# Delta-rule scan: both units of a head pair turned back to back, the output thread spread over four slots per pair

## The chip, the cores and the metric

One core of one Trainium2 chip runs the whole program. The metric is device time in microseconds of one execution, and the number given is the median over several executions. TensorE (PE in the profile) multiplies matrices into PSUM, and its loads of the stationary operand are listed as PEld. VectorE is DVE, ScalarE is ACT, GpSimd is POOL, SyncE is SP; SyncE issues the transfers of the part changed here. Each engine works through its own list of instructions in order and waits at semaphores that others raise.

## The reference, cut to what matters

The program computes two blocks of a network with some ten stages. The one that changes is the scan of the first block (RWKV branch): six heads of width 64, two directions, 256 context positions and then 2048 positions, each with a 64x64 state per head.

```python
def _rwkv_scan(state, ins, emit):
    r, w, k, v, kk, a = (jnp.moveaxis(z, 1, 0) for z in ins)
    xs = (w, k, v, kk, a, r) if emit else (w, k, v, kk, a)

    def step(S, inp):
        w_t, k_t, v_t, kk_t, a_t = inp[:5]
        sa = jnp.einsum('bhvk,bhk->bhv', S, kk_t)
        S = (S * w_t[:, :, None, :] - sa[..., None] * (kk_t * a_t)[:, :, None, :]
             + v_t[..., None] * k_t[:, :, None, :])
        y = jnp.einsum('bhvk,bhk->bhv', S, inp[5]) if emit else None
        return S, y
```

Context positions only move the state; for the others y is the result.

## The kernel before, in words

`rwkv_scan` (from line 1437) takes 128 positions of all heads and both directions in a pass, as two chunks of 64. There are NS = 18 passes, two for the context and 16 that give outputs. Heads stand in NG = 3 pairs g, and each pair has two units u = 2g and 2g + 1, one per direction (NU = 6). In each pass a small triangular system per head and chunk has to be inverted. This is done in five doubling levels for each of the three pairs, which makes NI = 15 items, and the pass is cut into 15 slots j, one per item. Three threads of work are laid into these slots, and every engine goes through the slots in the same written order, with the loop pass n:

- The **inverse thread** of pass n. In each slot TensorE does `asked` (line 1635, 16 matmuls, 32 at level 1) for item i and then `grown` (line 1661, 16 matmuls) for item i - 1. ScalarE copies what asked made (line 1775), and grown waits for that copy. VectorE takes what grown made with a predicated copy (line 1817), then transposes it for the next level (1823, 1825). An item's asked waits for the transposes of the item three slots before and, since the PSUM tile `inv` has two buffers, for the predicated copy of the item two before (of level 5: its whole result).
- The **output thread** of pass n - 1. For each pair: `solved` (line 1673, 16 matmuls, two ScalarE scalings behind it, lines 1781 and 1784), `moves` (1690, 16 matmuls, then the two VectorE additions into PQ, line 1833), `gains` (1700, 32 matmuls, then ScalarE's GY copy, line 1789). Each waits for what the one before left on the other engine, all through the PSUM tile `db`. After the third pair come two `state` halves (1711, up to 48 matmuls each), each followed by VectorE's additions into S and Y (1841, 1849). Slots 0 to 8 hold these nine groups and slots 9 and 10 the states.
- The **front thread** of pass n + 1. For each of six units: `turned` (line 1606) puts four 128x128 transposes into the PSUM tile `gram`, ScalarE copies them out (lines 1768, 1769), `grams` (1619, 24 matmuls) writes the same tile, and VectorE multiplies it with a mask into TK (line 1810). The next unit's turned waits for that mask. From slot 3 on, turned stands in slots 3, 5, ... 13 and grams in slots 4, 6, ... 14.

GpSimd scales the inputs that turned reads (`scaled`, 1571, tile XE with two buffers, so that it waits for the turned of two units before) and makes the start of the inverse from the masked grams (`start_of`, 1583), one unit at a time. SyncE loads the inputs of pass n + 3 (three buffers X) once VectorE has made PQ of the pair in pass n, and stores Y after both states.

Within a slot TensorE's order is: asked, grown, output group, front group. VectorE's is: predicated copy and transposes, PQ or state, mask. ScalarE's is: copy of asked, solved or gains, copies of turned.

Of the kernel before, what the change touches and what calls it, by code (L numbers as in the profile page):

```python
# [14 lines left out]
P = 128  # L15
# [1421 lines left out]
def rwkv_scan(nc, R, E, masks, levels, eye, ident, YR):  # L1437

    C = HD
    NG = MT_R  # L1440
    NU = 2 * NG
    NCX, NLT = CTX // P, SEQ // P
    NS = NCX + NLT
# [5 lines left out]
    HEADS = [slice(h * HD, (h + 1) * HD) for h in range(2)]  # L1449
    CHUNKS = [slice(c * C, (c + 1) * C) for c in range(2)]  # L1450
    LANES = [(cp, h) for h in range(2) for cp in range(2)]
    FIRST_HALF, SECOND_HALF = 3 * NG, 3 * NG + 1
    FRONTS_AT = 3

    with ExitStack() as ctx:
        s = Scope(nc, ctx, "rsc")
        X = [[s.sb(f"X{b}{u}", [P, 6, P]) for u in range(NU)] for b in range(3)]
# [39 lines left out]
        def front_banks(f):  # L1497

            return (inv[0], inv[1], db, gram, db, gram)[f] if f < NU else gram

        def other(t):

# [21 lines left out]
        with nc.Block() as block:  # L1524
# [44 lines left out]
            @block.gpsimd  # L1569
            def _(pool):  # L1570
                def scaled(n, u):

                    f = n * NU + u
                    x = X[n % 3][u]
                    pool.wait_ge(x_in[n % 3][u], (n // 3 + 1) * (96 if u % 2 == 0 else 64))
                    if f >= 2:
                        pool.wait_ge(tl_full, f - 1)
                    ends = e[:, u, 2 * n:2 * n + 2]
                    nc.gpsimd.tensor_tensor(x[:, X_I, :].rearrange("p (c t) -> p c t", c=2), ey[:].rearrange("p (c t) -> p c t", c=2),
                                            ends.unsqueeze(2).broadcast_to([P, 2, C]), ALU.mult)  # L1580
                    nc.gpsimd.tensor_tensor(XE[u % 2][:], x[:, X_KB:X_KB + 2, :], ends.unsqueeze(2).broadcast_to([P, 2, P]), ALU.mult).then_inc(xe_ready, 1)

                def start_of(n, u):

                    g, d = u // 2, u % 2
                    pool.wait_ge(m4_done, n * NU + u + 1)
                    tk = TK[n % 2][g]
                    nc.gpsimd.tensor_tensor(W[n % 2][g][:, d, :, :], tk[:, K_S0:K_AT - 1:-1, d, :], ey[:].unsqueeze(1).broadcast_to([P, 2, P]),
                                            ALU.add).then_inc(start_ready, 1)

                nc.gpsimd.memset(S[0][:], 0.0).then_inc(zeroed, 1)
                pool.wait_ge(const_in, 16 * 5)
                for n in range(NS):
                    scaled(n, 0)
                    scaled(n, 1)
                    for u in range(NU):
                        start_of(n, u)
                        if u + 2 < NU:
                            scaled(n, u + 2)

            @block.tensor
            def _(pe):
# [3 lines left out]
                def turned(n, u):  # L1606

                    f = n * NU + u
                    x, to = X[n % 3][u], front_banks(f)
                    pe.wait_ge(xe_ready, f + 1)  # L1610
                    if f >= NU:
                        pe.wait_ge(m4_done, f)
                    elif f >= 4:
                        pe.wait_ge(m4_done, f - 1)
                    for j, src in enumerate((x[:, X_AL, :], XE[u % 2][:, 0, :], XE[u % 2][:, 1, :], x[:, X_V, :])):
                        t = nc.tensor.transpose(to[:, 0, j * P:(j + 1) * P], src, idn[:])
                    t.then_inc(tl_full, 1)

                def grams(n, u):

                    f = n * NU + u
                    x, to = X[n % 3][u], front_banks(f)
                    pe.wait_ge(tl_done, f + 1)
                    for cp in range(2):
                        for h in range(2):
                            mm(to[:, h, cp * P:(cp + 1) * P], x[HEADS[h], X_KB + cp, :], alpha_rho(x, h, u, cp))
                    for cp, h in LANES:
                        be = slice(C, P) if cp == 0 else slice(0, C)
                        mm(to[other(CHUNKS[cp]), h, 4 * C:5 * C], x[HEADS[h], X_AL, rows_of(u % 2, CHUNKS[cp])], x[HEADS[h], X_KB + cp, be])
                    for cp, h in LANES:  # L1630
                        be, al = slice(C, P) if cp == 0 else slice(0, C), rows_of(u % 2, CHUNKS[cp])
                        last = mm(to[al, h, 5 * C:6 * C], x[HEADS[h], X_KB + cp, be], x[HEADS[h], X_AL, al])
                    last.then_inc(gram_full, 1)
# [111 lines left out]
                for n in range(NS + 1):  # L1745
                    for j in range(NI):
                        i = n * NI + j
                        if n < NS:
                            asked(i)
                        if 1 <= i <= NS * NI:  # L1750
                            grown(i - 1)
                        if n:
                            g, part = divmod(j, 3)
                            if j < FIRST_HALF:
                                (solved, moves, gains)[part](n - 1, g)
                            elif j <= SECOND_HALF:
                                state(n - 1, j - FIRST_HALF)
                        if j >= FRONTS_AT and n + 1 < NS:
                            u, part = divmod(j - FRONTS_AT, 2)
                            (turned, grams)[part](n + 1, u)  # L1760

            @block.scalar
            def _(act):
                def turned(n, u):
                    f = n * NU + u
                    act.wait_ge(tl_full, f + 1)
                    tk, to = TK[n % 2][u // 2], front_banks(f)[:, 0, :].rearrange("p (a t) -> p a t", a=4)
                    nc.scalar.copy(tk[:, K_AL:K_V + 1, u % 2, :], to)
                    nc.scalar.copy(tk[CHUNKS[1], K_V + 1, u % 2, :], to[CHUNKS[1], 3, :]).then_inc(tl_done, 1)

                def asked(i):
                    n, lev, g = item(i)
                    act.wait_ge(z_full, i + 1)
                    k = 2 if lev == 1 else 1
                    nc.scalar.copy(TK[n % 2][g][:, K_Z:K_Z + k, :, :].rearrange("p a u t -> p u a t"),
                                   inv[i % 2][:, :, 0:k * P].rearrange("p u (a t) -> p u a t", a=k)).then_inc(z_taken, 1)

                def solved(n, g):
                    act.wait_ge(x12_full, n * NG + g + 1)
                    made = db[:, :, 0:2 * P].rearrange("p u (h a k) -> p u h a k", h=2, a=2)  # L1780
                    nc.scalar.mul(XA[g][:], made[:, :, :, 0, :], -1.0)
                    for cp, t in enumerate(CHUNKS):
                        z = other(t)
                        last = nc.scalar.mul(TK[n % 2][g][z, K_V + cp, :, :].rearrange("p u (h k) -> p u h k", h=2), made[z, :, :, 1, :], -1.0)
                    last.then_inc(x12_ready, 1)

                def gains(n, g):
                    act.wait_ge(gy_full, n * NG + g + 1)
                    nc.scalar.copy(GY[:, g, :, :].rearrange("p (c x) k -> p c (x k)", c=2), db[:, :, 0:2 * P]).then_inc(gy_ready, 1)

                act.wait_ge(const_in, 16 * 5)
                for u in range(NU):
                    turned(0, u)
                for n in range(NS + 1):
                    for j in range(NI):
                        if n < NS:
                            asked(n * NI + j)
                        if n and j < FIRST_HALF and j % 3 != 1:
                            (solved, None, gains)[j % 3](n - 1, j // 3)
                        if j >= FRONTS_AT and n + 1 < NS and (j - FRONTS_AT) % 2 == 0:  # L1800
                            turned(n + 1, (j - FRONTS_AT) // 2)

            @block.vector
            def _(dve):
# [49 lines left out]
                for n in range(NS + 1):  # L1854
                    for j in range(NI):
                        i = n * NI + j
                        if 1 <= i <= NS * NI:
                            grown(i - 1)
                        if n and j < FIRST_HALF and j % 3 == 1:
                            moves(n - 1, j // 3)  # L1860
                        elif n and FIRST_HALF <= j <= SECOND_HALF:
                            state(n - 1, j - FIRST_HALF)
                        if j >= FRONTS_AT and n + 1 < NS and (j - FRONTS_AT) % 2:
                            grams(n + 1, (j - FRONTS_AT) // 2)


def hgrn(nc, PT, q0, i0, z0, masks, ident, head_ones, YH):
# [1966 lines left out]
```

## Time and profile before

| | us |
|---|---|
| median of 3 executions | 5530.79 |
| lowest, highest | 5526.96, 5538.92 |
| profiled execution, its own time | 5535.01 |
| span of its profile | 5533.2 |
| TensorE busy | 4917.3 (89%) |
| VectorE busy | 3518.4 (64%) |
| ScalarE busy | 1930.8 (35%) |
| GpSimd busy | 1292.0 (23%) |

The profiled execution lies 4.2 us above the median; its span leaves out 1.8 us around it. The busy shares are means over about ten stages with different limits. The scan lies between about 984 and 1660 us of the span. Busy time of TensorE counts each matmul from its start to its modelled end, so that neighbouring ones overlap. In the timeline, instructions of one line and tile that follow each other closely are one row: its first start, its length until the last end, and the count.

### The profile page before, as it was taken

What the parts mean: (1) busy time and instruction counts of PE and PEld (TensorE: products, weight loads), DVE (VectorE), ACT (ScalarE), POOL (GpSimd) and SP (SyncE); (2) the same over time, 40 slices, a digit from 0 to 9 for tenths busy, and PEclk for the clock granted to TensorE, in tenths of its full rate; (3) what the DMA queues carried; (4) which work ended last, traced back from release to release, by engine and by line L of the source; (5) the groups of instructions that cost most, each with busy time, mean ns of one, the idle gap of its engine ahead of it and who ended that gap; (6) DMA issues with size and microseconds to landing.
All of it is one profiled execution on the core that took longest, in us unless ns stands there. A gap on an engine that the chain in (4) does not pass through costs nothing. (4 is left out here: it accounts for less than half of the span.)

```text
span 5533.2 us, 113254 instructions
## 1 busy us (share of the span) xinstructions
PE 4917.3 (89%) x47505; PEld 3761.5 (68%) x47505; DVE 3518.4 (64%) x5799; ACT 1930.8 (35%) x3321; POOL 1292.0 (23%) x1130
## 2 busy tenths in 40 slices
PE   5999999799987866979998679999897999979989
PEld 2788888677776754858886334444486888766767
DVE  5166566577768874858982678888654000358877
ACT  3244444344435522341112234444304000136642
POOL 4111111222210000350000047677535111000012
PEclk7999999899998988989999779999998999979999
DMA  8244434322211124633324210000364112220145
GB/s 290 82 142 163 142 138 150 107 70 70 71 33 71 57 97 163 196 117 113 109 89 168 96 45 23 19 18 14 113 190 130 69 71 74 95 96 34 41 130 159
DMA packets 506325, 561.09 MB, mean 101 GB/s; under 512 B 114830, under 2 KB 411290, under 8 KB 493802
## 3 DMA queue, kind: packets, MB, share of 16 engines
q1 hardware_dynamic: 435900, 366.30, 21.7%
q10 hardware_dynamic: 54622, 130.36, 6.1%
q0 software_dynamic: 15312, 57.45, 2.6%
q8 instruction: 362, 5.93, 0.4%
q14 instruction: 129, 1.06, 0.1%
HBM read 350.86 MB, written 203.12 MB: 100 GB/s over the span
## 5 line engine op out<-in xcount | busy, mean ns | idle before, releaser
L164 PE MATMUL p_bank<-p_hT_high,p_w_high 128*128 128x512 f32 (+1 forms) x2744 | 1038.8, 379 | 7.8 <-PEq L37 7.8
L165 PE MATMUL p_bank<-p_hT_low,p_w_high 128*128 128x512 f32 (+1 forms) x2744 | 1030.6, 376 | 0.0
L166 PE MATMUL p_bank<-p_hT_high,p_w_low 128*128 128x512 f32 (+1 forms) x2744 | 1030.5, 376 | 0.0
L164 PEld LDWEIGHTS p_bank<-p_hT_high,p_w_high 128*128 128x128 f32 x2744 | 517.8, 189 | 109.6 <-issue 17.5
L166 PEld LDWEIGHTS p_bank<-p_hT_high,p_w_low 128*128 128x128 f32 x2744 | 518.0, 189 | 94.0
L165 PEld LDWEIGHTS p_bank<-p_hT_low,p_w_high 128*128 128x128 f32 x2744 | 518.3, 189 | 92.2
L3076 POOL TENSOR_TENSOR at_acc<-at_acc,at_p 128x512 f32<-128x512 f32 x256 | 414.4, 1619 | 125.0 <-ACT at_p L3012 102.3
L3012 ACT ACTIVATE at_p<-at_sc 128x1024 f32<-128x1024 f32 (+1 forms) x296 | 284.8, 1013 | 379.2 <-PE at_sc L2903 361.4
L3118 DVE TENSOR_REDUCE at_mx<-at_mb 128x2 f32<-128x1024 f32 (+1 forms) x280 | 342.1, 1222 | 51.8 <-PE at_mb L2914 51.5
L164 PE MATMUL o_bank<-o_w_high,o_m_high 128*128 128x512 f32 x800 | 315.3, 394 | 64.1 <-POOL o_m_low L158 64.1
L1050 DVE COPY p_o<-p_bank 128x512 f32<-128x512 f32 (+1 forms) x52 | 33.9, 651 | 466.8 <-PE p_bank L166 466.8
L165 PE MATMUL o_bank<-o_w_low,o_m_high 128*128 128x512 f32 x800 | 314.5, 393 | 0.0
L166 PE MATMUL o_bank<-o_w_high,o_m_low 128*128 128x512 f32 x800 | 314.1, 393 | 0.0
L2935 PE MATMUL at_ob<-at_p,at_V 128*64 128x512 f32 (+1 forms) x1184 | 283.4, 599 | 0.7 <-ACT at_osb L3019 0.7
L1604 PE MATMUL rsc_inv<-rsc_W,rsc_TK 64*64 64x64 f32 x8640 | 253.9, 222 | 8.4 <-DVE rsc_W L1817 6.9
L2902 PE MATMUL at_sc<-at_Q,at_K 128*128 128x512 f32 (+1 forms) x592 | 247.4, 419 | 1.9 <-DMA at_Q<-attention_tops 1.9
L413 ACT COPY p_o<-p_bank 128x512 f32<-128x512 f32 (+1 forms) x147 | 82.2, 560 | 477.8 <-PE p_bank L166 468.4
L1604 PEld LDWEIGHTS rsc_inv<-rsc_W,rsc_TK 64*64 64x64 f32 x8640 | 219.2, 135 | 35.4 <-issue 31.1
L3150 DVE TENSOR_TENSOR at_acc<-at_acc,at_p 128x512 f32<-128x512 f32 x256 | 205.2, 801 | 55.5 <-ACT at_p L3012 49.0
L2903 PE MATMUL at_sc<-at_Q,at_K 128*128 128x512 f32 (+1 forms) x592 | 232.2, 393 | 0.0
L164 PEld LDWEIGHTS o_bank<-o_w_high,o_m_high 128*128 128x128 f32 x800 | 152.2, 190 | 97.0 <-POOL o_m_low L158 65.2
L1134 ACT ACTIVATE p_eo<-p_bank 128x512 f32<-128x512 f32 (+1 forms) x100 | 55.6, 556 | 422.0 <-PE p_bank L166 422.0
(448 smaller groups left out, 9842.3 us busy)
## 6 DMA issues: line engine op xcount, KB each, us to landing
pT<-p_o ACTq DMA_DIRECT2D x128, 256.0 KB, 2.4
rwkv_chunks<-p_arr POOLq DMA_DIRECT2D x54, 512.0 KB, 5.4
o_z<-pT SPq DMA_DIRECT2D x50, 512.0 KB, 5.3
o_y<-y SPq DMA_DIRECT2D x50, 512.0 KB, 6.7
pT<-p_eo ACTq DMA_DIRECT2D x96, 256.0 KB, 2.0
rsc_X<-rwkv_chunks SPq DMA_DIRECT2D x378, 64.0 KB, 2.1
x<-o_o ACTq DMA_DIRECT2D x32, 512.0 KB, 2.7
o_x<-x SPq DMA_DIRECT2D x32, 512.0 KB, 4.6
```

Of the source, the lines that this page charges most:

```text
L164: nc.tensor.matmul(out, lhs[0], rhs[0], start=start, stop=False)
L165: nc.tensor.matmul(out, lhs[0], rhs[1], start=False, stop=False)
L166: return nc.tensor.matmul(out, lhs[1], rhs[0], start=False, stop=stop)
L413: nc.scalar.copy(o[x % NO][:, 0:cnt], ps[c][:, 0:cnt]).then_inc(b_free[c], 1)
L1604: return nc.tensor.matmul(out, l, r, start=start, stop=stop)
L2902: nc.tensor.matmul(sc[t % 2][:, h, 0:n], K1[kv][:, keys], Q1[b % NBUF][:, h, 0:n], start=True, stop=False)
L2903: m = nc.tensor.matmul(sc[t % 2][:, h, 0:n], K2[kv][:, keys], Q2[b % NBUF][:, h, 0:n], start=False, stop=True)
L2935: m = nc.tensor.matmul(ob[h * HD:(h + 1) * HD, 0:n], V[:, tiles[j], kv * HD:(kv + 1) * HD], pr[t % 4][:, h, 0:n], start=(j == 0), stop=(t ...
L3012: nc.scalar.activation(pr[t % 4][:, :, 0:n], sc[t % 2][:, :, 0:n], ACT.Exp, scale=SC).then_inc(exp_done, 1)
L3076: nc.gpsimd.tensor_tensor(acc[b % 2][:, 1, 0:n], acc[b % 2][:, 1, 0:n], pr[t % 4][:, 1, 0:n], ALU.add).then_inc(sum_b, 1)
L3118: r = nc.vector.reduce_max(mx[b % 2][:, :, t:t + nt, c], top_bank(m)[:, :, 0:nt * n].rearrange("p h (j k) -> p h j k", j=nt), AX)
L3150: nc.vector.tensor_tensor(acc[b % 2][:, 0, 0:n], acc[b % 2][:, 0, 0:n], pr[t % 4][:, 0, 0:n], ALU.add).then_inc(sum_a, 1)
```

## The change

The front thread now turns both units of a pair one right after the other, into the two banks of the `gram` tile (`turned_bank`), in slots 2, 6 and 10. Grams follow in slots 3, 4, 7, 8, 11 and 12. The grams of the even unit wait for the copies of both units, and those of the odd unit for the even unit's mask; the next pair's turned waits for the odd unit's mask. The output thread takes four slots per pair: solved, moves, gains in slots 0, 1, 2, then 4, 5, 6, then 8, 9, 10, and the states in slots 11 and 13. Slot 14 has neither. GpSimd scales the two units of the next pair before it makes the starts of this one. The grams' matmuls are as before, the first four of each unit on stationaries of 128 columns.

```diff
--- before.py
+++ after.py
@@ -1449,8 +1449,10 @@
     HEADS = [slice(h * HD, (h + 1) * HD) for h in range(2)]
     CHUNKS = [slice(c * C, (c + 1) * C) for c in range(2)]
     LANES = [(cp, h) for h in range(2) for cp in range(2)]
-    FIRST_HALF, SECOND_HALF = 3 * NG, 3 * NG + 1
-    FRONTS_AT = 3
+    OUTPUTS_AT = [4 * g + part for g in range(NG) for part in range(3)]
+    FIRST_HALF, SECOND_HALF = 4 * NG - 1, 4 * NG + 1
+    TURNED_AT = [4 * g + 2 for g in range(NG)]
+    GRAMS_AT = [4 * g + 3 + u for g in range(NG) for u in range(2)]
 
     with ExitStack() as ctx:
         s = Scope(nc, ctx, "rsc")
@@ -1498,6 +1500,10 @@
 
             return (inv[0], inv[1], db, gram, db, gram)[f] if f < NU else gram
 
+        def turned_bank(f):
+
+            return front_banks(f)[:, 0 if f < NU else f % 2, :]
+
         def other(t):
 
             return slice(C, P) if t.start == 0 else slice(0, C)
@@ -1590,13 +1596,17 @@
 
                 nc.gpsimd.memset(S[0][:], 0.0).then_inc(zeroed, 1)
                 pool.wait_ge(const_in, 16 * 5)
+                scaled(0, 0)
+                scaled(0, 1)
                 for n in range(NS):
-                    scaled(n, 0)
-                    scaled(n, 1)
-                    for u in range(NU):
-                        start_of(n, u)
-                        if u + 2 < NU:
-                            scaled(n, u + 2)
+                    for g in range(NG):
+                        for d in range(2):
+                            if g + 1 < NG:
+                                scaled(n, 2 * g + 2 + d)
+                            elif n + 1 < NS:
+                                scaled(n + 1, d)
+                        for d in range(2):
+                            start_of(n, 2 * g + d)
 
             @block.tensor
             def _(pe):
@@ -1606,21 +1616,27 @@
                 def turned(n, u):
 
                     f = n * NU + u
-                    x, to = X[n % 3][u], front_banks(f)
+                    x, to = X[n % 3][u], turned_bank(f)
                     pe.wait_ge(xe_ready, f + 1)
                     if f >= NU:
-                        pe.wait_ge(m4_done, f)
+                        if u % 2 == 0:
+                            pe.wait_ge(m4_done, f)
                     elif f >= 4:
                         pe.wait_ge(m4_done, f - 1)
                     for j, src in enumerate((x[:, X_AL, :], XE[u % 2][:, 0, :], XE[u % 2][:, 1, :], x[:, X_V, :])):
-                        t = nc.tensor.transpose(to[:, 0, j * P:(j + 1) * P], src, idn[:])
+                        t = nc.tensor.transpose(to[:, j * P:(j + 1) * P], src, idn[:])
                     t.then_inc(tl_full, 1)
 
                 def grams(n, u):
 
                     f = n * NU + u
                     x, to = X[n % 3][u], front_banks(f)
-                    pe.wait_ge(tl_done, f + 1)
+                    if f < NU:
+                        pe.wait_ge(tl_done, f + 1)
+                    elif u % 2 == 0:
+                        pe.wait_ge(tl_done, f + 2)
+                    else:
+                        pe.wait_ge(m4_done, f)
                     for cp in range(2):
                         for h in range(2):
                             mm(to[:, h, cp * P:(cp + 1) * P], x[HEADS[h], X_KB + cp, :], alpha_rho(x, h, u, cp))
@@ -1750,21 +1766,25 @@
                         if 1 <= i <= NS * NI:
                             grown(i - 1)
                         if n:
-                            g, part = divmod(j, 3)
-                            if j < FIRST_HALF:
-                                (solved, moves, gains)[part](n - 1, g)
-                            elif j <= SECOND_HALF:
-                                state(n - 1, j - FIRST_HALF)
-                        if j >= FRONTS_AT and n + 1 < NS:
-                            u, part = divmod(j - FRONTS_AT, 2)
-                            (turned, grams)[part](n + 1, u)
+                            if j in OUTPUTS_AT:
+                                (solved, moves, gains)[j % 4](n - 1, j // 4)
+                            elif j == FIRST_HALF:
+                                state(n - 1, 0)
+                            elif j == SECOND_HALF:
+                                state(n - 1, 1)
+                        if n + 1 < NS:
+                            if j in TURNED_AT:
+                                turned(n + 1, 2 * (j // 4))
+                                turned(n + 1, 2 * (j // 4) + 1)
+                            elif j in GRAMS_AT:
+                                grams(n + 1, GRAMS_AT.index(j))
 
             @block.scalar
             def _(act):
                 def turned(n, u):
                     f = n * NU + u
                     act.wait_ge(tl_full, f + 1)
-                    tk, to = TK[n % 2][u // 2], front_banks(f)[:, 0, :].rearrange("p (a t) -> p a t", a=4)
+                    tk, to = TK[n % 2][u // 2], turned_bank(f).rearrange("p (a t) -> p a t", a=4)
                     nc.scalar.copy(tk[:, K_AL:K_V + 1, u % 2, :], to)
                     nc.scalar.copy(tk[CHUNKS[1], K_V + 1, u % 2, :], to[CHUNKS[1], 3, :]).then_inc(tl_done, 1)
 
@@ -1795,10 +1815,11 @@
                     for j in range(NI):
                         if n < NS:
                             asked(n * NI + j)
-                        if n and j < FIRST_HALF and j % 3 != 1:
-                            (solved, None, gains)[j % 3](n - 1, j // 3)
-                        if j >= FRONTS_AT and n + 1 < NS and (j - FRONTS_AT) % 2 == 0:
-                            turned(n + 1, (j - FRONTS_AT) // 2)
+                        if n and j in OUTPUTS_AT and j % 4 != 1:
+                            (solved, None, gains)[j % 4](n - 1, j // 4)
+                        if j in TURNED_AT and n + 1 < NS:
+                            turned(n + 1, 2 * (j // 4))
+                            turned(n + 1, 2 * (j // 4) + 1)
 
             @block.vector
             def _(dve):
@@ -1856,12 +1877,14 @@
                         i = n * NI + j
                         if 1 <= i <= NS * NI:
                             grown(i - 1)
-                        if n and j < FIRST_HALF and j % 3 == 1:
-                            moves(n - 1, j // 3)
-                        elif n and FIRST_HALF <= j <= SECOND_HALF:
-                            state(n - 1, j - FIRST_HALF)
-                        if j >= FRONTS_AT and n + 1 < NS and (j - FRONTS_AT) % 2:
-                            grams(n + 1, (j - FRONTS_AT) // 2)
+                        if n and j in OUTPUTS_AT and j % 4 == 1:
+                            moves(n - 1, j // 4)
+                        elif n and j == FIRST_HALF:
+                            state(n - 1, 0)
+                        elif n and j == SECOND_HALF:
+                            state(n - 1, 1)
+                        if j in GRAMS_AT and n + 1 < NS:
+                            grams(n + 1, GRAMS_AT.index(j))
 
 
 def hgrn(nc, PT, q0, i0, z0, masks, ident, head_ones, YH):
```

## Rows read from the trace of the kernel before

**Rows 1.** Windows: us, busy us (instructions) of PE, PEld, DVE, ACT, POOL, clock, DMA.

```profile
984.00:1020.00 36.00, 16.08 (x176) 12.21 (x180) 4.79 (x5) 5.09 (x12) 9.50 (x18) 0.55 0.62 177
...
1055.00:1600.00 545.00, 500.40 (x15308) 433.78 (x15306) 421.97 (x1048) 253.17 (x612) 154.92 (x281) 1.00 0.26 68
```

**Rows 2.** Waits of TensorE in the steady scan, 1060 to 1600: total, times, longest.

```profile
PE rsc_gram L1616 <- DVE rsc_TK L1810: 18.5, 31, 0.7
```

**Rows 3.** Timeline of TensorE, one pass: start us, us, line, count, idle before.

```profile
1326.05 0.41 PE L1604 MATMUL rsc_inv<-rsc_W,rsc_TK 64*64 64x64 f32 x16
...
1326.94 0.23 PE L1604 MATMUL rsc_inv<-rsc_W,rsc_TK 64*64 64x64 f32 x2
...
1327.80 0.46 PE L1604 MATMUL rsc_inv<-rsc_W,rsc_TK 64*64 64x64 f32 x16 [0.20 <-DVE rsc_W L1817]
...
1331.36 1.20 PE L1604 MATMUL rsc_db<-rsc_TK 128*64 128x64 f32 x32 [0.53 <-DVE rsc_PQ L1833]
1332.49 0.91 PE L1604 MATMUL rsc_inv<-rsc_W,rsc_TK 64*64 64x64 f32 x32
...
1338.88 0.33 PE L1616 MATMUL rsc_gram<-rsc_idn,rsc_X 128*128 128x128 f32 x1
...
1339.27 0.27 PE L1616 MATMUL rsc_gram<-rsc_idn,rsc_X 128*128 128x128 f32 x1
1339.47 0.86 PE L1604 MATMUL rsc_inv<-rsc_W,rsc_TK 64*64 64x64 f32 x30
...
1340.75 1.11 PE L1604 MATMUL rsc_gram<-rsc_X 64*128 64x128 f32 x24
1341.68 0.70 PE L1604 MATMUL rsc_inv<-rsc_W,rsc_TK 64*64 64x64 f32 x26
...
1345.07 1.20 PE L1604 MATMUL rsc_db<-rsc_TK 128*64 128x64 f32 x32 [0.56 <-DVE rsc_PQ L1833]
...
1347.13 0.87 PE L1604 MATMUL rsc_inv<-rsc_W,rsc_TK 64*64 64x64 f32 x32
1347.84 0.87 PE L1604 MATMUL rsc_db<-rsc_S,rsc_PQ 64*64 64x64 f32 x24
...
1349.33 0.33 PE L1616 MATMUL rsc_gram<-rsc_idn,rsc_X 128*128 128x128 f32 x1
...
1352.17 1.11 PE L1604 MATMUL rsc_gram<-rsc_X 64*128 64x128 f32 x24
1353.09 0.87 PE L1604 MATMUL rsc_inv<-rsc_W,rsc_TK 64*64 64x64 f32 x32
1354.45 0.30 PE L1616 MATMUL rsc_gram<-rsc_idn,rsc_X 128*128 128x128 f32 x1 [0.49 <-DVE rsc_TK L1810]
...
1355.01 0.92 PE L1604 MATMUL rsc_inv<-rsc_W,rsc_TK 64*64 64x64 f32 x32
1356.03 1.11 PE L1604 MATMUL rsc_gram<-rsc_X 64*128 64x128 f32 x24
1356.95 0.87 PE L1604 MATMUL rsc_inv<-rsc_W,rsc_TK 64*64 64x64 f32 x32
1358.55 0.30 PE L1616 MATMUL rsc_gram<-rsc_idn,rsc_X 128*128 128x128 f32 x1 [0.72 <-DVE rsc_TK L1810]
...
1361.05 0.41 PE L1604 MATMUL rsc_inv<-rsc_W,rsc_TK 64*64 64x64 f32 x16
```

**Rows 4.** Timeline of ScalarE, same pass: behind the gains of slot 5.

```profile
1338.99 0.59 ACT L1789 COPY rsc_GY<-rsc_db 128x512 f32<-128x512 f32 x1 [1.19 <-PE rsc_db L1604]
1339.58 0.59 ACT L1768 COPY rsc_TK<-rsc_gram 128x512 f32<-128x512 f32 x1
1340.17 0.26 ACT L1769 COPY rsc_TK<-rsc_gram 64x128 f32<-64x128 f32 x1
```

**Rows 5.** Timeline of VectorE, same pass: mask of slot 6, PQ of slot 7.

```profile
1341.93 0.96 DVE L1810 TENSOR_TENSOR rsc_TK<-rsc_gram,rsc_mk 128x768 f32<-128x768 f32 x1
...
1344.26 0.76 DVE L1833 TENSOR_TENSOR rsc_PQ<-rsc_db,rsc_X 128x256 f32<-128x256 f32 x2
```

## The prediction, made before the changed kernel was run

> **What bounds the kernel now.** Only the delta-rule scan changes, so I first asked for busy time by stretch [rows 1]. In the 545 us of steady scan TensorE is busy 500 us at a granted clock of 1.00, VectorE 422, ScalarE 253, GpSimd 155. "Busy 500" isn't work, since the records of pipelined matmuls overlap; the question is how often TensorE's next group starts late. The waits [rows 2] show one such place by name, the turned tiles behind VectorE's mask: 31 times, 0.6 us each. The timeline of one pass then gives the rest [rows 3]. Passes repeat: 1326.05 to 1361.05 is 35.00 us, 15 slots. I took from it what each group costs when it doesn't wait, from its start to the start of the next:
> - asked + grown (in every slot): 0.70 (1347.13 to 1347.84, rounded down)
> - with the solved group behind them 1.28 (1339.47 to 1340.75)
> - gains 1.13 (1331.36 to 1332.49)
> - one half of the state 1.49 (1347.84 to 1349.33)
> - turned 0.59 (1338.88 to 1339.47)
> - grams 0.93 (1340.75 to 1341.68, and 1352.17 to 1353.09).
>
> Then the late starts. Slot 11: ready at 1353.09 + 0.70 = 1353.79, turned at 1354.45: 0.66 late. Slot 13: 1356.95 + 0.70 = 1357.65, turned at 1358.55: 0.90 late. Slot 12: 1355.01 + 0.70 = 1355.71, grams at 1356.03: 0.32 late, behind ScalarE's copy, and slot 14 is built like it. Together 2.2 us in a pass: the front thread (turned, copy, grams, mask, next turned) has no output group beside it there. The change removes these. The gains of slots 2 and 8 also start late, for PQ (the bracketed 0.53 and 0.56 are only the visible part).
>
> **The change part by part**, walked through a new pass from 0.
>
> *Slots 0 to 2.* Same groups in the same order up to the end of the first gains: 1326.05 to 1332.49, 6.44 us [rows 3]. The change takes nothing out here.
>
> *Turned, twice, behind the gains (slots 2, 6, 10).* Per pass it is six groups as before. TensorE then needs asked and grown, and wants grams of the even unit, which now wait for BOTH copies, and ScalarE has the gains' GY copy before them in its queue. The existing chain is [rows 4]: gains end on TensorE 1338.88, GY from 1338.99, turned's copies from 1339.58 to 1340.17 + 0.26 = 1340.43, 1.55 after the gains' end. A second pair of copies repeats 1340.43 - 1339.58 = 0.85 plus some 0.03 between, and a copy is seen by TensorE 0.06 after it ends: 1.55 + 0.88 + 0.06 = 2.50 us from the gains' end to grams. TensorE's own work in that time is two turned (1.03, below), asked and grown 0.70: 1.73. A new wait of 0.77, in slots 3 and 7; behind it asked and grown of the next slot stand as well. In slot 11 the half state (1.49) covers it.
> The two turned without anything between: from first to last transpose 1338.88 to 1339.27, 0.39, spaced 0.11 after the first, and 0.20 from the last to the next group. So 0.39 + 0.11 + 0.33 + 0.20 = 1.03 where two single ones take 1.18. In slots 2 and 6 ScalarE decides the end, so this counts once in a pass.
> That saving has a rule behind it: the Trainium skill's "TensorEngine Tiling (Array Packing)", Key Properties, says that changing the tiling mode drains TensorE, and a turned is a 128x128 group between 64-row groups. Counted by the rule alone the change would save 0.15 three times instead of once, and the end would be some 5 us earlier; the copies' rows speak against that.
>
> *Grams to grams.* The odd unit's grams wait for the even unit's mask. That chain exists now as grams to the next turned: 1352.17 to 1354.45, 2.28 us [rows 3]. Cover in slots 3 to 4 is 0.93 + 1.28 (asked, grown, solved) = 2.21, so 0.07 is left. In slots 11 to 12 it is 0.93 + 0.70, so 0.65.
>
> *Odd grams to gains.* The new order puts moves in slot 5 and gains in slot 6 behind grams of slot 4. VectorE takes them in order: mask, copy and transposes of a level, PQ. The same order exists in slots 6 to 8 now: grams 1340.75, mask at 1341.93 [rows 5], PQ 1344.26 + 0.76 = 1345.02, gains at 1345.07: 4.32 us. Nothing in it was waiting for TensorE longer than for VectorE (the mask starts right after the grams), so I take 4.32 again, though TensorE has one turned (0.59) less to do in it and so waits longer. It happens twice now (gains of pairs 1 and 2) instead of once. In the old pass the gains of pair 1 hardly waited, since their mask came behind PQ.
>
> *Slots 13 and 14.* Slot 14 holds asked and grown only. The next asked needs the predicated copy of what that grown made. The price is in slot 0 to 1: last grown matmul 1326.94, asked 1327.80, 0.86 with the solved group in between, so solved hid 0.4 of it. Now nothing hides it.
>
> *Sum of a pass.* Slots 0 to 2: 6.44. Then twice (2.50 + 2.28 + 4.32 + 1.13 = 10.23): 20.46. Then turned twice 1.03, asked and grown 0.70, state 1.49, grams to grams 2.28, grams 0.93, asked and grown 0.70, state 1.45, asked and grown 0.70, wait 0.85: 10.13. In all 37.03 against 35.00: **2.0 us longer**. There are 16 passes with outputs and fronts: 32.5 us. The pass without outputs gains nothing and loses about 0.4 (bare slots in the middle), the two context passes have shorter states and lose about 0.1 more each, the last loop pass without fronts gives back 0.2. The tail has the same chain in both. **+33 us.**
>
> *Costed at nothing.* GpSimd: the same two kinds of instructions in another order; it is busy 155 of 545 us [rows 1], and the start tiles of the last pair are ready two slots earlier than now. SyncE: loads for the pass after next but one are released by PQ of pairs 1 and 2, one and two slots later, and the output store behind the second half state three slots later; all are needed a whole pass (35 us) on. If that cover were gone, each late load would hold up turned. The grams' matmuls (24 per unit) don't change at all, and the prologue only swaps a GpSimd order.
>
> *Bounds of the unseen.* The new neighbours moves-asked and state-asked were in no row; they lie beside waits, so between 0 and -0.15 each. The second pair of copies: between 0.85 (back to back) and 1.3, if the level's copy slipped ahead, which the program's order excludes; I take 0.88. The slot 14 wait: between 0.4 (part hidden) and 0.9. Per pass that is -0.7 to +0.5, in all -11 to +8.
>
> **The rivals.**
> 1. *Faster.* The front thread is the only thing that matters: 2.2 us of late starts leave each pass and the new waits don't come, because the four slots per pair give VectorE time. 16 x 2.2 = 35 us less, 5496. For it: these waits are the ones the profile names [rows 2]. Its point of decision is slot 6: PQ would have to be done 3.0 us after the odd grams' start; rows 3 and 5 show 4.32. Chance 5 in 100.
> 2. *No change.* The gains' waits fall to today's size in one of the two pairs and slot 14's is hidden by the asked group's first half: 2.2 gone, about as much new. 5531 +- 11. For it: VectorE has 123 us of slack in 545. Against: this slack lies in other slots. Chance 7.
> 3. *More waits than I see, the same kind:* the slots' asked groups too wait for VectorE's backlog, another 1 us per pass: 5580. Chance 12.
> 4. *The clock.* The granted clock is 1.00 with 4 transposes at a time and gaps under 1 us [rows 1]; before the scan, from 984 to 1020, with little matmul work, it is 0.55. If eight transposes and a 0.8 us wait let it drop to the lower level (1.2 GHz) around each pair, turned twice, asked, grown and grams (1.03 + 0.70 + 0.93 = 2.66) would take double, 8 us per pass, 128 us more: about 5690. The Trainium skill's "TensorE: Matmul & The Clock Gate", Part 4, says that transposes don't count as activity for the clock. Six turned per pass at 1.00 now speak against its mattering. Chance 2.
>
> That the change doesn't do what it says is no rival: the order of the groups is written out, and the wait conditions follow it. Only "128-column stationaries" changes no instruction.
>
> **How the numbers follow.** The forecast (74 in 100): the profiled execution took 5535.0 us, 4.2 above the median of the runs shown, so 5535.0 + 33 = 5568 for it and 5530.8 + 33 = **5564** for the median. Its own range is -11 to +8 from the unseen costs and some 6 of scatter between runs: 5550 to 5577. With the third rival the range is 5547 to 5582; it leaves out the first two and the clock. A measurement of this kernel can tell 0.2%, 11 us, from no change. Slower by more than that: forecast, rivals 3 and 4: 0.88. Within: 0.07. Faster: 0.05.
>
> **What would show it.** Right: a pass of 37.0 us; no wait of turned for the mask; in slots 3 and 7 grams 2.5 us after the gains' end, released by the copy L1769; gains of pairs 1 and 2 at 4.3 us after the odd grams' start, released by PQ; asked of slot 0 with 0.85 us before it. Wrong: a pass at or under 35.2; PQ less than 3.5 us behind the grams; a granted clock under 0.95 in the steady stretch; turned waiting for GpSimd.

## The result and the profile after

The changed kernel takes 5564.84 us in the median of 6 runs (5556.26 to 5570.34), the kernel before beside it 5533.68 (5523.72 to 5544.09, 6 runs). The ratio is 1.0055 with a 95% interval of 1.0039 to 1.0071: slower by 0.55%, clear of the 0.2% that can be told from nothing. The forecast was 5564 in 5547 to 5582. So the total is right, but it holds two items that nearly cancel and that the forecast had put at nothing or had no term for; they come below.

The steady scan, by windows (us, busy us of PE, PEld, DVE, ACT, POOL, granted clock, DMA share, GB/s), answers to [rows 1]:

```profile
1055.00:1600.00 545.00, 460.61 (x14238) 404.65 (x14233) 392.45 (x977) 239.14 (x571) 147.35 (x264) 0.99 0.25 65
```

In the same 545 us TensorE got through 14238 matmuls where it was 15308 before, 7% fewer, at nearly the same clock. Each pass with outputs has the same matmuls, so a pass takes longer. All waits of TensorE in the steady scan (total us, times, longest) answer to [rows 2]:

```profile
PE rsc_inv L1614 <- DVE rsc_W L1838: 28.4, 63, 0.6
PE rsc_db L1614 <- DVE rsc_PQ L1854: 27.2, 41, 0.8
PE rsc_gram L1614 <- ACT rsc_TK L1789: 15.9, 29, 0.5
PE rsc_gram L1614 <- DVE rsc_TK L1831: 5.8, 14, 0.6
PE rsc_inv L1614 <- issue: 5.6, 5, 1.5
```

Of two of these waits the kernel before had smaller ones, beside the row in [rows 2]:

```profile
PE rsc_db L1604 <- DVE rsc_PQ L1833: 16.8, 31, 0.6
PE rsc_inv L1604 <- DVE rsc_W L1817: 3.0, 15, 0.2
```

The old wait, turned (L1616 before, L1627 now) for the mask, is gone as the change meant it to be. Four new or grown ones stand in its place: asked for VectorE's predicated copy (3.0 before, 28.4 now), gains for PQ (16.8 before, 27.2 now), grams for ScalarE's copies, and the odd grams for the even unit's mask. The fifth, "issue", names no releaser.

One pass on TensorE (start us, length, line, count, idle before and its releaser), which answers to [rows 3]:

```profile
1382.24 0.46 PE L1614 MATMUL rsc_inv<-rsc_W,rsc_TK 64*64 64x64 f32 x16 [0.63 <-DVE rsc_W L1838]
...
1388.63 0.33 PE L1627 MATMUL rsc_gram<-rsc_idn,rsc_X 128*128 128x128 f32 x1
...
1389.66 0.92 PE L1614 MATMUL rsc_inv<-rsc_W,rsc_TK 64*64 64x64 f32 x32
1391.12 1.11 PE L1614 MATMUL rsc_gram<-rsc_X 64*128 64x128 f32 x24 [0.55 <-ACT rsc_TK L1789]
...
1393.31 1.11 PE L1614 MATMUL rsc_gram<-rsc_X 64*128 64x128 f32 x24
...
1396.07 0.92 PE L1614 MATMUL rsc_inv<-rsc_W,rsc_TK 64*64 64x64 f32 x32 [0.53 <-DVE rsc_W L1838]
1397.75 1.20 PE L1614 MATMUL rsc_db<-rsc_TK 128*64 128x64 f32 x32 [0.77 <-DVE rsc_PQ L1854]
1398.88 0.33 PE L1627 MATMUL rsc_gram<-rsc_idn,rsc_X 128*128 128x128 f32 x1
...
1409.13 0.33 PE L1627 MATMUL rsc_gram<-rsc_idn,rsc_X 128*128 128x128 f32 x1
...
1412.40 1.11 PE L1614 MATMUL rsc_gram<-rsc_X 64*128 64x128 f32 x24
...
1414.59 1.11 PE L1614 MATMUL rsc_gram<-rsc_X 64*128 64x128 f32 x24 [0.39 <-DVE rsc_TK L1831]
1415.52 0.87 PE L1614 MATMUL rsc_inv<-rsc_W,rsc_TK 64*64 64x64 f32 x32
...
1419.13 0.46 PE L1614 MATMUL rsc_inv<-rsc_W,rsc_TK 64*64 64x64 f32 x16 [0.64 <-DVE rsc_W L1838]
```

The pass is 1419.13 - 1382.24 = 36.89 us. It reads as the walk had it, section by section (predicted in brackets): slots 0 to 2 up to the end of the gains 6.39 (6.44); gains' end to grams 1391.12 - 1388.63 = 2.49 (2.50); grams to grams 2.19 (2.28); odd grams to gains 1397.75 - 1393.31 = 4.44 (4.32); gains 1.13 (1.13); the next pair the same, 1398.88 to 1409.13 = 10.25 (10.23); the rest of the pass 10.00 (10.13). The two turned in a row take 1389.66 - 1388.63 = 1.03, as predicted.

ScalarE and VectorE in that pass show why. ScalarE (same columns), behind the gains, answers to [rows 4]:

```profile
1388.74 0.58 ACT L1809 COPY rsc_GY<-rsc_db 128x512 f32<-128x512 f32 x1 [1.29 <-PE rsc_db L1614]
1389.33 0.58 ACT L1788 COPY rsc_TK<-rsc_gram 128x512 f32<-128x512 f32 x1
1389.93 0.26 ACT L1789 COPY rsc_TK<-rsc_gram 64x128 f32<-64x128 f32 x1
1390.21 0.58 ACT L1788 COPY rsc_TK<-rsc_gram 128x512 f32<-128x512 f32 x1
1390.81 0.26 ACT L1789 COPY rsc_TK<-rsc_gram 64x128 f32<-64x128 f32 x1
```

The five run with hardly a gap (0.03 us at most) from 1388.74 to 1391.07, and grams start 0.05 later, at 1391.12. VectorE answers to [rows 5]:

```profile
1394.62 0.96 DVE L1831 TENSOR_TENSOR rsc_TK<-rsc_gram,rsc_mk 128x768 f32<-128x768 f32 x1
1395.50 0.43 DVE L1838 COPY_PREDICATED rsc_W<-rsc_lv,rsc_inv 128x256 f32<-128x256 uint32 x1
...
1396.94 0.76 DVE L1854 TENSOR_TENSOR rsc_PQ<-rsc_db,rsc_X 128x256 f32<-128x256 f32 x2
```

Mask, the level's copy and transposes, PQ: 3.08 us in one line from 1394.62, and the gains start 0.05 after its end. TensorE has nothing else that its order allows.

### The profile page after: what moved, and what is told of

Same layout as the page of the kernel before. It is cut to its first block and busy times, and to the rows that moved or that the text cites. A ratio compares the mean times of both kernels' runs of the same rounds, so it can differ in the third digit from the quotient of the medians.

```text
span 5561.0 us, 113203 instructions
## 1 busy us (share of the span) xinstructions
PE 4907.5 (88%) x47505; PEld 3757.5 (68%) x47505; DVE 3514.4 (63%) x5799; ACT 1932.5 (35%) x3321; POOL 1294.9 (23%) x1130
## 3 DMA queue, kind: packets, MB, share of 16 engines
q14 instruction: 130, 1.06, 0.1%
## 5 line engine op out<-in xcount | busy, mean ns | idle before, releaser
L1614 PE MATMUL rsc_inv<-rsc_W,rsc_TK 64*64 64x64 f32 x8640 | 257.9, 222 | 43.8 <-DVE rsc_W L1838 38.6
L1838 DVE COPY_PREDICATED rsc_W<-rsc_lv,rsc_inv 128x256 f32<-128x256 uint32 x270 | 118.6, 439 | 153.1 <-PE rsc_inv L1614 150.0
```

The source lines that it names most:

```text
L1614: return nc.tensor.matmul(out, l, r, start=start, stop=stop)
L1838: made = nc.vector.copy_predicated(wt[:, :, 0, :], lv[:, lev, :, 0, :].bitcast(mybir.dt.uint32), new)
```

## The experiments

Passes are given from the second half of a pass's first asked (its matmuls `rsc_inv<-rsc_TK`) to that of the next. In each profile I take the commonest value among the passes that give outputs.

**e1, the pair without the slots.** The changed kernel, GpSimd's new order included, with the output thread where it was (ScalarE's and VectorE's loops change alike; TensorE's is shown):

```diff
-    OUTPUTS_AT = [4 * g + part for g in range(NG) for part in range(3)]
-    FIRST_HALF, SECOND_HALF = 4 * NG - 1, 4 * NG + 1
+    FIRST_HALF, SECOND_HALF = 3 * NG, 3 * NG + 1
...
-                            if j in OUTPUTS_AT:
-                                (solved, moves, gains)[j % 4](n - 1, j // 4)
+                            if j < FIRST_HALF:
+                                (solved, moves, gains)[j % 3](n - 1, j // 3)
```

> The changed kernel with the output thread back in slots 0 to 10 (solved, moves, gains in nine slots running, states in 9 and 10). Walk theory: turning both units together is the costly half. Walked with the same durations a pass takes 36.3 us, between before (35.0) and the changed kernel (36.9), and the kernel is about 21 us slower than before less what the start gains (6 us). Rival (four slots per pair are the costly half, since they leave slot 14 bare and put gains behind the mask): a pass of about 35, and no difference from before.

Measured: 5551.06 us against 5534.79, ratio 1.0030 (1.0017 to 1.0042), passes of 36.3. Both are what the walk gave (36.3 and 15 us net). Turning both units together, alone, adds 1.4 us to a pass, where the whole change adds 2.0.

**e2, the slots without the pair.** The kernel before with the output thread on the new slots on all engines, GpSimd and fronts as they were (the engines' loops, which follow these lists, are left out, in e4 too):

```diff
-    FIRST_HALF, SECOND_HALF = 3 * NG, 3 * NG + 1
+    OUTPUTS_AT = [0, 1, 2, 4, 5, 6, 8, 9, 10]
+    FIRST_HALF, SECOND_HALF = 11, 13
```

> The kernel before with only the output thread on four slots per pair (states in 11 and 13); fronts one unit at a time in slots 3 to 14, GpSimd's order as before. Walk theory: this half alone helps a little, since slots 11 and 13 get the states as cover for the mask: a pass of 34.7 us, the kernel 5 us faster, which the clock can't tell from no change. Rival (the output slots are the costly half): a pass of 36 or more, 15 us or more slower.

Measured: 5529.13 against 5534.79, ratio 0.9986 (0.9976 to 0.9996), passes of 34.6. A pass is 0.3 shorter than before. So the slots alone help a little, and it is only with the pair that they hurt: 36.9 with both, 36.3 with the pair alone. The two halves don't add up. It isn't the mask in front of PQ that the pair adds: e2 has that too, in both pairs, from the grams of slot 4 to the gains of slot 6 and from slot 8 to 10 (in the first 1296.37 to 1300.68, 4.31 us), and its gains wait 24.1 us for PQ in all, where the changed kernel's wait 27.2. What e2 hasn't got is any wait of the grams for ScalarE's copies (15.9 in the changed kernel), and its asked waits 3.0 us for the predicated copy and not 28.4. In e2 a turned stands between those grams and gains, under VectorE's chain; with the pair none does, and the asked and the gains wait instead.

**e3, grams one slot later.** The changed kernel with

```diff
-    GRAMS_AT = [4 * g + 3 + u for g in range(NG) for u in range(2)]
+    GRAMS_AT = [4 * g + 4 + u for g in range(NG) for u in range(2)]
```

> The changed kernel with both grams of a pair one slot later (slots 4, 5, 8, 9, 12, 13). Walk theory: the copies have ended when grams come, and the odd mask no longer stands before PQ on VectorE: a pass of 34.9 us against 36.9, 2.0 less, so about as fast as before. Rival (only the wait for the two copies costs): 1.5 less, 35.4. Rival (the pair's eight transposes and ScalarE's load cost whatever follows): 36.5 or more.

Measured: 5530.83 against 5534.79, ratio 0.9996 (0.9986 to 1.0005), passes of 35.0: 1.9 shorter than the changed kernel, from one line. It is the length that the theory gave (34.9) and not that of the copies' wait alone (35.4), and the transposes or ScalarE's load, both unchanged, can't hold 1.9 us. TensorE, from the first gains to the next:

```profile
1291.50 0.33 PE L1627 MATMUL rsc_gram<-rsc_idn,rsc_X 128*128 128x128 f32 x1
...
1294.08 0.93 PE L1614 MATMUL rsc_inv<-rsc_W,rsc_TK 64*64 64x64 f32 x30 [0.64 <-DVE rsc_W L1838]
...
1295.44 1.11 PE L1614 MATMUL rsc_gram<-rsc_X 64*128 64x128 f32 x24
...
1297.62 1.11 PE L1614 MATMUL rsc_gram<-rsc_X 64*128 64x128 f32 x24
1298.55 0.87 PE L1614 MATMUL rsc_inv<-rsc_W,rsc_TK 64*64 64x64 f32 x32
1299.75 0.46 PE L1614 MATMUL rsc_db<-rsc_TK 128*64 128x64 f32 x8 [0.33 <-DVE rsc_PQ L1854]
```

These gains end at 1300.88, so from the end of one pair's gains to that of the next it is 9.38 us where the changed kernel has 10.25. This comes twice in a pass; the rest of the pass gives 0.15. The grams' wait for the copies (0.55 visible) is gone, but the asked ahead of them now waits 0.64 for the predicated copy, so nothing is won there. What is won lies behind the grams: the wait of slot 6's asked (0.53) is gone, and the gains wait 0.33 for PQ and not 0.77. Between a pair's even grams and its PQ VectorE now has one mask to do and not two; the odd unit's mask comes behind PQ. Two rows of TensorE's waits:

```profile
PE rsc_inv L1614 <- DVE rsc_W L1838: 35.2, 62, 0.8
PE rsc_db L1614 <- DVE rsc_PQ L1854: 15.9, 42, 0.5
```

The gains' wait for PQ fell from 27.2 to 15.9 us, and the wait of grams for ScalarE (15.9) isn't among the rows any more. The wait of asked for VectorE has grown in its place (28.4 to 35.2), in the slot between turned and grams that is now bare.

**e4, other slots.** The same walk, used to look for a better order. The kernel before with

```diff
-    FIRST_HALF, SECOND_HALF = 3 * NG, 3 * NG + 1
-    FRONTS_AT = 3
+    OUTPUTS_AT = [0, 1, 2, 3, 4, 6, 7, 8, 10]
+    FIRST_HALF, SECOND_HALF = 12, 13
+    TURNED_AT, GRAMS_AT = [2, 4, 6, 8, 10, 12], [3, 5, 7, 9, 11, 14]
```

> The kernel before with other slots: outputs in 0, 1, 2, 3, 4, 6, 7, 8, 10, states in 12 and 13, turned one unit at a time in 2, 4, 6, 8, 10, 12, grams in 3, 5, 7, 9, 11, 14. Walk theory: nearly every mask and copy has another group beside it, a pass takes 32.7 us against 35.0, 16 times 2.3 is 37 us less: 5495. Rival (TensorE's own issue is the bound at about 35 once waits are moved, or late instruction fetches grow as it issues faster): a pass of 34 or more, less than 16 us gained.

Measured: 5505.35 against 5534.79, ratio 0.9939 (0.9922 to 0.9955), 29 us less. The steady scan by windows, and TensorE's waits there:

```profile
1055.00:1600.00 545.00, 520.47 (x16106) 453.03 (x16103) 445.39 (x1109) 268.94 (x643) 157.14 (x284) 1.00 0.26 68
```

```profile
PE rsc_inv L1605 <- DVE rsc_W L1821: 6.4, 21, 1.1
PE rsc_db L1605 <- DVE rsc_PQ L1837: 5.3, 11, 0.5
PE rsc_inv L1605 <- issue: 2.5, 6, 1.1
PE rsc_db L1605 <- issue: 1.9, 4, 0.7
```

16106 matmuls in the window, 5% more than before. One pass goes from 1244.54 to 1277.30, 32.76 us; the walk had 32.7. But other passes of it take up to 34.3, and the mean of fourteen is 33.1. The 37 us expected came out as 29 mostly for that reason. The rows hold 4.4 us of "issue", waits with no releaser; that late instruction fetches are behind them is not shown. The rival as it stood, a pass of 34 or more and less than 16 us gained, is out.

**e5, GpSimd's order alone.** The start of the scan had become shorter by 6.2 us in the changed kernel (29.8 against 36.1 from the stage's begin, at 985.8 and 984.2, to the second half of the first asked), and the forecast had put it at nothing.

```diff
+                scaled(0, 0)
+                scaled(0, 1)
                 for n in range(NS):
-                    scaled(n, 0)
-                    scaled(n, 1)
-                    for u in range(NU):
-                        start_of(n, u)
-                        if u + 2 < NU:
-                            scaled(n, u + 2)
+                    for g in range(NG):
+                        for d in range(2):
+                            if g + 1 < NG:
+                                scaled(n, 2 * g + 2 + d)
+                            elif n + 1 < NS:
+                                scaled(n + 1, d)
+                        for d in range(2):
+                            start_of(n, 2 * g + d)
```

> The kernel before with GpSimd's new order alone (the next pair is scaled before this pair's starts). Theory: this order makes up the whole shorter start of the scan, 6.2 us less from the stage's begin to the first asked (29.8 against 36.1), and a steady pass stays at 34.9; in all 6 us. Rival (the start is shorter because turned now stands in pairs): the start stays at 36 us. Rival (GpSimd's order also matters in the steady passes): a pass differs from 34.9 by more than 0.2.

Measured in one run: 5534.87 us beside a median of 5535.81, which can't tell 6 us. The profile can: the start is 28.1 us, so 8.0 shorter and not 6.2; steady passes are 34.9 as before. Waits of TensorE from 999 to 1019 behind the one long wait for the first inputs (19.1 and 19.6 us), first the kernel before, then e5:

```profile
PE rsc_db L1616 <- POOL rsc_XE L1581: 2.9, 2, 1.9
PE rsc_gram L1616 <- POOL rsc_XE L1581: 1.5, 2, 0.8
```

```profile
PE rsc_inv L1608 <- DVE rsc_W L1821: 1.3, 2, 0.6
PE rsc_db L1608 <- ACT rsc_TK L1773: 0.5, 1, 0.5
```

In the first pass nothing hides GpSimd. Scaling unit 2 stood behind the start of unit 0, and this behind the mask of unit 0, so TensorE's turned of later units waited for inputs that could have been ready. With the new order that wait is gone, 4.4 us. The rival that gave it to the pair falls: here turned is as before.

The rest goes with the clock. From the first turned to the first asked, by windows (us, busy us of PE, PEld, DVE, ACT, POOL, granted clock, DMA share, GB/s), the kernel before, e5, and e8 below, which has the same GpSimd order:

```profile
999.40:1019.80 20.40, 15.88 (x168) 11.98 (x172) 4.79 (x5) 5.09 (x12) 7.78 (x15) 0.58 0.54 139
1000.60:1012.70 12.10, 10.88 (x168) 8.53 (x171) 4.58 (x5) 5.08 (x12) 9.30 (x18) 0.86 0.57 146
1002.20:1017.60 15.40, 15.03 (x164) 11.72 (x168) 4.56 (x5) 5.07 (x12) 9.25 (x18) 0.56 0.56 140
```

At about the clock of the kernel before (0.56 and 0.58) the new order saves 5.0 us; the 3.3 us between e8 and e5 go with the granted clock. The changed kernel has 14.3 us at 0.67 there. What sets the clock in this stretch no run takes apart.

**e6, the changed kernel again, and e7, with 64 more instructions of TensorE in front.** In the changed kernel's profile four passes were longer than 36.9: the 3rd 37.5, the 6th 39.8, the 10th 39.5, the 15th 38.3. In each, TensorE's stream stops inside the asked and grown of slot 1, with nobody named that it waits for.

> The changed kernel as it is, looked at again. In its profile passes 3, 6, 10 and 15 of the scan were 0.6 to 2.9 us longer, with a gap of 1.4 to 1.7 us in TensorE's stream in slots 0 and 1, for which the profile knows no releaser, each just behind a 16 KB instruction fetch. Fetch theory: the place of a fetch in the program is fixed, so the gaps come again in slots 0 to 2 of mostly the same passes, with sizes that vary. Rival (a disturbance from outside): gaps at other places, or none.

```diff
+                for _ in range(16):
+                    nc.tensor.transpose(inv[0][:, 0, 0:P], idn[:], idn[:])
+                for _ in range(16):
+                    nc.tensor.transpose(inv[0][:, 0, P:2 * P], idn[:], idn[:])
                 for u in range(0, NU, 2):
                     turned(0, u)
```

> The changed kernel with 32 more 128x128 transposes (64 instructions of TensorE with their weight loads) ahead of the scan's first turned, into a PSUM tile that is overwritten later. Fetch theory: the block borders lie 64 instructions elsewhere in a pass, so the passes with gaps of over 1.2 us are others than 3, 6, 10 and 15, and the normal pass stays at 36.9. Rival (the gaps belong to transfers or to the passes themselves): the same passes as before.

Measured: e6 has the same four long passes, 37.2, 38.1, 38.8 and 38.2, and no other above 37.1. In both profiles the stops stand at the same places, 2.4, 2.6, 2.3 and 2.7 us behind the first asked of the pass. e7 has none of the four; its long ones are the 7th (38.6) and the 16th (38.2), and every other full pass stays between 36.9 and 37.1. (One run each: 5570.09 and 5560.60.) So the place in the program decides, not the pass, the transfers of that pass or chance. The gaps in the 10th pass of e6 and the 7th of e7:

```profile
1343.58 0.21 PE L1614 MATMUL rsc_inv<-rsc_TK 64*64 64x64 f32 x1 [1.69 <-issue]
```

```profile
1228.71 0.28 PE L1614 MATMUL rsc_inv<-rsc_W,rsc_TK 64*64 64x64 f32 x3 [1.47 <-issue]
```

**e8, the slots of e4 with GpSimd's order of e5.** Both edits above on the kernel before.

> The kernel with the replaced slots of e4 and GpSimd's new order. If the two add up, it is 6 us faster than e4: about 5499 beside a before of 5534, with a start of some 30 us and passes of 32.8 us. Rival (with turned in slot 2 the next pair's inputs, scaled earlier, change nothing or collide): the time of e4.

Measured: 5503.07 against 5535.81, ratio 0.9937 (0.9924 to 0.9949); start 31.3 us, and passes whose commonest length I can't give, since they scatter from 32.8 to 34.4 (mean 33.3). This is 33 us less than before and 62 less than the changed kernel. Against e4 the start came 4.9 us earlier and the longer passes took 2 back, so the medians differ by 2 us, which is within the intervals, and not by the 6 expected. Its median is the lowest of all that ran.

## Why the prediction was right, point by point

- **The new waits.** Right in kind, place and size. The copies' chain, 2.50 predicted, is 2.49 and ends with L1789. The mask in front of PQ, 4.32 predicted, is 4.44. The slots alone have that chain too (e2, 4.31) and a shorter pass, so the price is that the pair leaves less beside it; e3, which puts the odd unit's mask behind PQ, gives the 1.9 us back. Slot 14's bare asked waits (0.63 and 0.64 visible, 0.85 counted from the last grown matmul).
- **Grams to grams** was sized from the wait of turned for a mask, 2.28; it is 2.19, so in slots 3 to 4 no wait is left and in slot 12 it is 0.56 instead of 0.65. A pass is 36.89, not 37.03.
- **The turned pair.** 1.03 as worked out. The Trainium skill's "TensorEngine Tiling (Array Packing)", Key Properties, says that a change of tiling mode drains TensorE. The trace agrees as far as it goes: two in a row take 0.15 less than two apart; no run here shows that the drain is the cause. The saving earned nothing in slots 2 and 6, as ScalarE's end set the grams.
- **The stage's sum.** From begin to end the scan takes 712.5 us where it took 678.4: 34.1 more. The forecast said 33. It is made of: steady passes, fourteen times 36.89 - 34.96 = 27.0; the two context passes without their long part 4.7 (36.24 - 33.91 twice, where some 2.1 each was forecast); four long passes 8.3 (7.0 among the fourteen, 1.3 in the second context pass); the first pass 0.9 (0.4 was forecast); the tail -0.4; and the start -6.2.
- **Two terms that failed.** "GpSimd ... costed at nothing", with the words "the prologue only swaps a GpSimd order": the start is worth -6.2 us, of which the order gives about 5 (e5 and e8 against the kernel before) and the rest goes with the clock. The cover I named for GpSimd is there in steady passes alone. And no term stood for the four long passes: +8.3. The stops themselves are 6.2 of it (1.4, 1.7, 1.7 and 1.5); some 2 us more are in the 6th and 10th pass, 2.9 and 2.6 longer, where the clock fell behind the stop. They cancel within 2 us, so the total is better than the reasons deserve.
- **The rest of the program.** Behind the scan the changed kernel's profile is 7.9 us shorter than the profile of before (3862.7 against 3870.6), in stages that the change doesn't touch. The other profiles spread over the same span there (e2 3865.0, e4 3873.7, e6 3872.2), so this is scatter and I give it no cause. With it, and a scan that begins 1.6 us later, the 34.1 us make the 27.8 by which the two profiles' spans differ; the medians differ by 31.2.
- **The rivals.** Faster and no change were out: PQ's end was not at 3.0 us but at 4.4 after the odd grams. A general backlog of 1 us more wasn't there. The clock came in, but small and elsewhere than this rival had it: in the changed kernel it did fall twice to the lower level (1.2 GHz), for 3.4 us each, in the 6th and 10th pass. The windows before, in and after the second fall:

```profile
1345.00:1348.30 3.30, 1.62 (x61) 1.27 (x56) 0.76 (x3) 1.13 (x3) 0.00 (x0) 1.00 0.05 9
1348.40:1351.70 3.30, 3.30 (x75) 3.09 (x65) 2.63 (x8) 0.59 (x1) 0.00 (x0) 0.50 0.11 30
1351.80:1355.00 3.20, 2.65 (x56) 2.23 (x60) 1.21 (x4) 2.65 (x6) 1.90 (x4) 1.00 0.46 125
```

  Both times it followed a gap of 1.7 us in slot 1 (at 1194.8 and 1345.0), not a pair of turned, and in e6 a gap of 1.9 us passed without a fall. Ahead of the fall TensorE had waited in slots 14, 0 and 1 as well. Everywhere else in the steady scan the pairs of turned kept the full level. The Trainium skill's "TensorE: Matmul & The Clock Gate", Part 4, says that the full clock doesn't engage for transposes, which don't count as busy in the same way; the rows show the pairs at 1.00, and no run here shows a price for that.

## What to carry to other kernels

In a program of written-out slots, take one pass from the timeline, note in it each group's length without a wait, each chain between engines from its own rows, and walk a new order with them: five orders were forecast that way to within 0.15 us of their commonest pass, of 33 to 37. In these orders what counted was what each in-order queue had in front of the thing that is awaited, here masks in front of PQ and copies in front of grams, and what the other engine had to do meanwhile. Where little waiting is left the walk promises too much: e4's mean pass is 0.4 us above the walked one. Price the first pass on its own, since there nothing covers a slow helper.

## What the runs showed of the hardware that I had not expected

Instructions come over a queue of their own in 16 KB blocks, one in 4 to 5 us of the steady scan. The profile doesn't say for which engine; that they are TensorE's is my reading, from the stops that follow some of them. Here is what was on the queues between 1343.6 and 1347 in the changed kernel, around the gap at 1345.0 (packets, MB, share of 16 engines):

```profile
q1 hardware_dynamic: 435, 0.21, 22.5%
q8 instruction: 1, 0.02, 3.1%
```

The block started at 1343.7 and took 1.69 us, the longest of the 139 in the scan (median 1.06). In the changed kernel the block in question started 0.6 to 1.3 us before the stream stopped, in all four long passes, and the stream stood still for 1.4 to 1.7 us (from the last matmul's start to the next one's; the brackets in the rows count from its modelled end, 0.2 us less). All these gaps lie where TensorE goes through 48 small matmuls and their weight loads in asked and grown of one slot. But most passes have a block starting in slots 0 to 2, in the kernel before too, and lose 0.2 us at most. So a start there is not enough. Nor are crowded transfers needed: between the block's start and the stop the DMA engines' share was 0.54 in the 10th pass, as above, but 0.05 to 0.07 in the other three. I read it as a fetch asked for too late for so fast a stretch; e6 and e7 show only that the place in the program decides. What tips it, and whether the length of a fetch sets the size of the gap, stays open. In e4 and e8, where TensorE waits least, more passes are long by 0.3 to 1.7 us.
